# A two-layer decoder trunk on one core: first-layer scale and shift as columns by matmuls with stationary weights, in place of rows that are turned

## The reference

```python
def modulate(h, shift, scale):
    return h * (1 + scale[:, None, :]) + shift[:, None, :]

c_act = jax.nn.silu(c)
for l in range(DEPTH):
    mod = c_act @ w_ada[l] + b_ada[l]
    sh1, sc1, g1, sh2, sc2, g2, sh3, sc3, g3 = jnp.split(mod, N_MOD, axis=-1)
    h = modulate(rmsnorm(x, norm_ffn1[l]), sh1, sc1)
    x = x + 0.5 * g1[:, None, :] * swiglu(h, ffn1_w_up[l], ffn1_w_down[l])
    ...
```

## Time and profile before

| | us |
|---|---|
| median of 3 runs | 2423.11 |
| lowest and highest | 2422.92, 2424.08 |
| profiled execution, its own time | 2424.26 |
| span of the profiled execution | 2422.5 |

### The profile page before, as it was taken

How to read it: one execution, slowest core, us unless ns; L and a number is a source line. 1 busy time by engine, 2 the same in 40 slices (tenths; PEclk the granted TensorE clock), 3 DMA queues, 4 the chain that set the end, 5 groups by cost and what they waited for, 6 DMA issues and landing times.

```text
span 2422.5 us, 34408 instructions
## 1 busy us (share of the span) xinstructions
PE 2405.7 (99%) x11560; PEld 1981.8 (82%) x11560; DVE 1496.8 (62%) x2297; ACT 879.7 (36%) x1388; POOL 213.3 (9%) x159
## 2 busy tenths in 40 slices
PE   8999999999999999999999999999999999999999
PEld 6888888888888888888888888888888888888887
DVE  5777778687744577443577677877785446533332
ACT  4222223556432342222332222346653323421233
POOL 0032012000012000010300000200100111000001
PEclk9999999999999999999999999999999999999999
DMA  9666654322245346343346566533222453332332
GB/s 290 193 191 180 199 177 153 87 62 69 64 119 147 96 130 188 116 122 114 103 127 194 175 198 200 164 123 86 61 70 78 113 147 96 96 108 83 98 106 83
DMA packets 509615, 315.22 MB, mean 130 GB/s; under 512 B 9240, under 2 KB 503144, under 8 KB 508904
## 3 DMA queue, kind: packets, MB, share of 16 engines
q1 hardware_dynamic: 441376, 246.72, 35.0%
q10 hardware_dynamic: 68168, 67.62, 9.0%
HBM read 308.02 MB, written 6.29 MB: 130 GB/s over the span
## 4 chain that ended last, share of the span: by engine, by line
PE 97%; DVE 2%; ACT 0%; ACTq 0%; issue 0%
PE ps_proj L1838 28%; PE ps_proj L1839 28%; PE ps_proj L1840 28%; PE ps_mid L2074 1%; PE ps_mid L2076 1%; PE ps_mid L2075 1%; PE ps_o L2044 1%; PE ps_mid L2021 1%; PE ps_small L2033 1%; PE ps_mid L1838 1%; PE ps_mid L1840 1%; PE ps_mid L1839 1%; DVE sb_scratch L1064 1%; DVE sb_w_lo L1052 0%; PE ps_mid L2133 0%; DVE sb_h_lo L1133 0%
## 5 line engine op out<-in xcount | busy, mean ns | idle before, releaser
L1838 PE MATMUL ps_proj<-sb_a_hi,sb_w_hi 128*128 128x512 f32 x1878 | 731.2, 389 | 0.0
L1840 PE MATMUL ps_proj<-sb_a_hi,sb_w_lo 128*128 128x512 f32 x1878 | 730.7, 389 | 0.0
L1839 PE MATMUL ps_proj<-sb_a_lo,sb_w_hi 128*128 128x512 f32 x1878 | 730.6, 389 | 0.0
L609 ACT ACTIVATE sb_w_hi<-sb_raw 128x1024 fp32r<-128x1024 f32 (+1 forms) x382 | 424.5, 1111 | 829.1 <-PE ps_proj L1840 780.2
L1052 DVE TENSOR_TENSOR sb_w_lo<-sb_raw,sb_w_hi 128x1024 fp32r<-128x1024 f32 (+1 forms) x384 | 504.6, 1314 | 304.4 <-ACT sb_w_hi L609 303.6
L1838 PE MATMUL ps_proj<-sb_h_hi,sb_w_hi 128*128 128x512 f32 x1194 | 470.4, 394 | 0.1
L1840 PE MATMUL ps_proj<-sb_h_hi,sb_w_lo 128*128 128x512 f32 x1194 | 465.1, 389 | 0.0
L1839 PE MATMUL ps_proj<-sb_h_lo,sb_w_hi 128*128 128x512 f32 x1194 | 465.0, 389 | 0.0
L1840 PEld LDWEIGHTS ps_proj<-sb_a_hi,sb_w_lo 128*128 128x128 f32 x1878 | 352.4, 188 | 73.2
L1839 PEld LDWEIGHTS ps_proj<-sb_a_lo,sb_w_hi 128*128 128x128 f32 x1878 | 352.6, 188 | 73.0
L1838 PEld LDWEIGHTS ps_proj<-sb_a_hi,sb_w_hi 128*128 128x128 f32 x1878 | 352.5, 188 | 73.0
(11 more groups left out here) (297 smaller groups left out, 1938.9 us busy)
## 6 DMA issues: line engine op xcount, KB each, us to landing
sb_raw<-in_ffn_w_up SPq DMA_DIRECT2D x172, 512.0 KB, 3.8
sb_scratch<-in_w_ada ACTq DMA_DIRECT2D x128, 512.0 KB, 4.4
sb_raw<-in_w_in SPq DMA_DIRECT2D x100, 512.0 KB, 3.9
sb_raw<-in_ffn_w_down SPq DMA_DIRECT2D x64, 704.0 KB, 4.8
sb_raw<-in_w_branch_swa SPq DMA_DIRECT2D x16, 512.0 KB, 3.8
sb_raw<-in_w_branch_ret SPq DMA_DIRECT2D x16, 512.0 KB, 3.9
sb_raw<-in_w_out SPq DMA_DIRECT2D x16, 512.0 KB, 3.8
sb_scratch<-in_w_ada SPq DMA_DIRECT2D x6, 1024.0 KB, 10.5
```

The costliest lines, as they stand in the source:

```text
L609: act.activation(Whi[s][:, 0:n], raw[s][:, 0:n], ACT.Copy).then_inc(hi_ready, 1)
L1838: pe.matmul(bank, Whi[s][:, w], hi, start=first, stop=False)
L1839: pe.matmul(bank, Whi[s][:, w], lo, start=False, stop=False)
L1840: return pe.matmul(bank, Wlo[s][:, w], hi, start=False, stop=last)
```

## The change

- PE makes columns directly. `first_cols(g)` takes each 128 x 128 piece of a w_ada block as the stationary operand and one column of silu(c) as the moving one: for each of the two blocks of a group, two output columns of eight accumulating matmuls. That is 32 matmuls for a group where `first_rows` had 16, and the copies on ACT, the transposes on PE and the sums of parts on DVE are gone. `first_columns(g)` on DVE is one addition of biases for scale and shift together, read from PSUM, and one operation for the gain.
- `first_cols(g + 1)` stands where both `first_rows` of the next group stood. `first_cols(0)` stands after all turns of x.
- c is issued first on SP, ahead of x, and no more second on ACT. `idle(5)` becomes `idle(4)`.
- In the turns of x, DVE copies tiles 0, 1, 4, 5 and ACT tiles 2, 3, 6, 7 (before: even and odd ones), and the spread of 1/rms stands before tiles 6 and 7.
- In group 0, DVE makes both lo parts of the weights before the lo parts of the tiles.

```diff
-            def first_rows(n):
-
-                tile, bank = first_raw[n % FIRST_BUFS], row_banks[n % 2]
-                pe.wait_ge(first_in[n], 16)
-                if n > 1:
-                    pe.wait_ge(row_copied, n - 1)
-                for r in range(KT):
-                    a = r % ROW_GROUPS
-                    last = pe.matmul(bank[32 * a:32 * (a + 1), :], c_act[:, r:r + 1].broadcast_to([P, 32]), tile[:, 256 * r:256 * (r + 1)],
-                                     start=(r < ROW_GROUPS), stop=(r >= ROW_GROUPS))
-                last.then_inc(first_used, 1)
-
-            def turn_rows(n):
...
+            def first_cols(g):
+
+                if g:
+                    pe.wait_ge(cols_made, g)
                 else:
                     pe.wait_ge(cols_done, 1)
...
+                for kind in (SCALE, SHIFT):
+                    n = block_no(g, kind)
+                    tile = first_raw[n % FIRST_BUFS]
+                    pe.wait_ge(first_in[n], 16)
+                    for j in range(2):
+                        for r in range(KT):
+                            last = pe.matmul(pS[:, 2 * kind + j:2 * kind + j + 1], tile[:, 256 * r + P * j:256 * r + P * (j + 1)], c_act[:, r:r + 1],
+                                             start=(r == 0), stop=(r == KT - 1))
+                    last.then_inc(first_used, 1)
...
-            idle(5)
+            idle(4)
...
+            turn_x(range(4))
+            turn_vectors()
+            turn_x((4, 5))
...
             spread_rstd(0, pO, 0).then_inc(rb_ready, 1)
-            turn_rows(SCALE)
+            turn_x((6, 7))
+            first_cols(0)
             pe.wait_ge(xt_dve, KT // 2)
             pe.wait_ge(xt_act, KT // 2)
-            first_rows(SHIFT)
-            turn_rows(SHIFT)
...
                             if more:
-                                first_rows(2 * g + 2 + SCALE)
-                                first_rows(2 * g + 2 + SHIFT)
+                                first_cols(g + 1)
...
-                                elif n == 0:
-                                    turn_rows(2 * g + 2 + SCALE)
-                                    turn_rows(2 * g + 2 + SHIFT)
```

```diff
+            sp.dma_start(vec_rows[0:8, 0, :], c.rearrange("b (k p) -> (b k) p", p=P)).then_inc(c_in, 16)
             for t in range(TT):
                 sp.dma_start(xtok[:, t, :], x[0, P * t:P * (t + 1), :]).then_inc(x_in[t], 16)
...
             act.dma_start(K[:, 0:K_DECAY], consts[:, 0:K_DECAY]).then_inc(const_in, 16)
-            act.dma_start(vec_rows[0:8, 0, :], c.rearrange("b (k p) -> (b k) p", p=P)).then_inc(const_in, 16)
...
-                copy_first_row(2 * g + SCALE)
-                copy_first_row(2 * g + SHIFT)
...
+            def first_columns(g):
+
+                cols = pS[:, 0:4].rearrange("p (n j) -> p n j", n=2)
+                dve.wait_ge(first_used, 2 * (g + 1))
+                two = [a[:, 0:2 * KT].rearrange("p (n k) -> p n k", k=KT)[:, :, 2 * g:2 * g + 2] for a in (mod, vcols[:, 64:64 + 2 * KT])]
+                st.mark(dve.tensor_tensor(two[0], cols, two[1], ALU.add))
                 st.wait()
...
+                at, col = KT + 2 * g, GAIN_COL["ffn1"] + 2 * g
+                dve.scalar_tensor_tensor(gain[:, 2 * g:2 * g + 2], mod[:, at:at + 2], 1.0, vcols[:, col:col + 2], ALU.add, ALU.mult).then_inc(cols_made, 1)
+                dve.wait_ge(cols_made, g + 1)
```

More of the change, by code:

```diff
@@ L50 @@
 JOBS, FIRST_JOBS, FIRST_PAIRS = 36, 8, 2
-FIRST_BUFS, ROW_GROUPS = 4, 4
-GROUPS, SCALE, SHIFT = KT // 2, 0, 1
+FIRST_BUFS = 4
+X_DVE, X_ACT = (0, 1, 4, 5), (2, 3, 6, 7)
+GROUPS, SHIFT, SCALE = KT // 2, 0, 1
 HALF_JOBS = (JOBS - FIRST_JOBS) // 2
@@ L207, in decoder @@
         turn_banks = [pA[0], pA[1], pM[:, 0, :], pM[:, 1, :]]
-        row_banks, row_turns = [pM[:, 2 + n, 0:256] for n in range(2)], [pS[:, 256 * n:256 * (n + 1)] for n in range(2)]
         pair_banks = [pA, [pM[:, 0, :], pM[:, 1, :]]]
@@ L212, in decoder @@
         x_spill = nc.dram_tensor("x_spill", [P, KT * T], F, kind="Internal").ap()
-        const_in, vec_in, tables_in = sem("const_in"), sem("vec_in"), sem("tables_in")
+        const_in, c_in, vec_in, tables_in = sem("const_in"), sem("c_in"), sem("vec_in"), sem("tables_in")
         x_in = [sem(f"x_in{t}") for t in range(TT)]
@@ L222, in decoder @@
         first_w_in = [sem(f"first_w_in{n}") for n in range(2 * GROUPS)]
-        first_used, row_copied, row_turned, cols_made = (sem(n) for n in ("first_used", "row_copied", "row_turned", "cols_made"))
+        first_used, cols_made = sem("first_used"), sem("cols_made")
         first_w_hi, first_w_lo, xn_shifted = sem("first_w_hi"), sem("first_w_lo"), sem("xn_shifted")
@@ L347, in in_last_layer, with block_no @@
                 work()
+        def block_no(g, kind):
+            return 2 * g + (0 if kind == SCALE else 1)
         block = ctx.enter_context(nc.Block())
@@ L493, in _ @@
             st = Steps(pool, pool_step)
-            pool.wait_ge(const_in, 16 * 2)
+            pool.wait_ge(const_in, 16)
             pool.wait_ge(pos_in, 16)
@@ L841, in copy_x @@
                 act.activation(XV[:, k, :], turn_banks[k % 4][:, :], ACT.Copy).then_inc(xt_act, 1)
-            def copy_first_row(n):
-                act.wait_ge(first_used, n + 1)
-                if n > 1:
-                    act.wait_ge(row_turned, n - 1)
-                act.activation(first_row[n % 2], row_banks[n % 2], ACT.Copy).then_inc(row_copied, 1)
             def first_weights(g):
@@ L862, in _ @@
             act.activation(rs_t[:, 0:TT], rs_v[:, 0:TT], ACT.Sqrt).then_inc(first_root, 1)
-            for k in range(1, KT, 2):
+            for k in X_ACT:
                 copy_x(k)
             for g in range(GROUPS):
-                if g:
-                    first_weights(g)
-                copy_first_row(2 * g + SCALE)
-                copy_first_row(2 * g + SHIFT)
-                if g == 0:
-                    first_weights(g)
+                first_weights(g)
                 for kk in range(2):
@@ L1425, in copy_x @@
                 dve.tensor_copy(XV[:, k, :], turn_banks[k % 4][:, :]).then_inc(xt_dve, 1)
[L1427 to L1431, removed]
-                st.wait()
[L1433 to L1440, removed]
+            def first_columns(g):
[3 more added lines that the diff above has]
+                st.mark(dve.tensor_tensor(two[0], cols, two[1], ALU.add))
+                st.wait()
+                at, col = KT + 2 * g, GAIN_COL["ffn1"] + 2 * g
+                dve.scalar_tensor_tensor(gain[:, 2 * g:2 * g + 2], mod[:, at:at + 2], 1.0, vcols[:, col:col + 2], ALU.add, ALU.mult).then_inc(cols_made, 1)
+                dve.wait_ge(cols_made, g + 1)
             def scaled_x(k):
@@ L1462, in _ @@
             y, a, v = rstd[:, 0:TT], rs_t[:, 0:TT], rs_v[:, 0:TT]
-            copy_x(0)
+            for k in X_DVE[0:2]:
+                copy_x(k)
             dve.wait_ge(ssq_done, TT)
             dve.tensor_scalar(v, ssq, 1.0 / D, EPS, ALU.mult, ALU.add).then_inc(first_v, 1)
-            copy_x(2)
             dve.wait_ge(first_root, 1)
@@ L1474, in _ @@
             dve.scalar_tensor_tensor(y, a, 1.5, y, ALU.add, ALU.mult).then_inc(rstd_ready, 1)
-            copy_x(4)
-            copy_x(6)
+            for k in X_DVE[2:4]:
+                copy_x(k)
             dve.wait_ge(cols_ps, 1)
@@ L1480, in _ @@
             dve.wait_ge(xt_act, KT // 2)
+            dve.wait_ge(xt_ps, KT)
             dve.wait_ge(rb_ready, 1)
-            scaled_x(0)
             dve.wait_ge(cols_done, 1)
-            first_columns(0, SCALE)
-            scaled_x(1)
+            for k in range(2):
+                scaled_x(k)
             for g in range(GROUPS):
@@ L1489, in _ @@
                         first_weights(g, s)
-                    first_columns(g, SCALE)
-                first_columns(g, SHIFT)
+                first_columns(g)
                 st.wait()
@@ L1496, in _ @@
                 shifted_x(2 * g + 1)
-                first_lo(2 * g)
                 if g == 0:
                     first_weights(g, 1)
-                first_lo(2 * g + 1)
+                for kk in range(2):
+                    first_lo(2 * g + kk)
                 if g < GROUPS - 1:
-                    scaled_x(2 * g + 2)
-                    scaled_x(2 * g + 3)
+                    for kk in range(2):
+                        scaled_x(2 * g + 2 + kk)
             for s in range(2):
@@ L1761, in _ @@
             pe.sem_inc(y_ps, 1)
-            pe.wait_ge(const_in, 16 * 2)
+            pe.wait_ge(const_in, 16)
+            pe.wait_ge(c_in, 16)
             pe.transpose(pO[:, 0:KT], vec_rows[0:KT, 0, :], ident[0:KT, 0:KT]).then_inc(c_ps, 1)
             pe.wait_ge(c_done, 1)
-            def first_rows(n):
-                tile, bank = first_raw[n % FIRST_BUFS], row_banks[n % 2]
-                pe.wait_ge(first_in[n], 16)
-                if n > 1:
-                    pe.wait_ge(row_copied, n - 1)
-                for r in range(KT):
```

(31 more changed lines are left out.)

1 line of the change is left out of this document (removed).

## The result

The changed kernel takes 2457.99 us (median of 4 runs, 2456.27 to 2459.77) against 2423.55 us before (4 runs, 2422.92 to 2424.08). The ratio is 1.0143 with a 95% interval of 1.0130 to 1.0155. It is slower by 34.4 us, where 12.7 were forecast. The profiled execution took 2457.26 us, 33.0 more than that of before, with a span of 2455.2.

A forecast was written before the change was run, and what follows sets the result against it. PE was taken as the bound, its block behind about 50 us moving whole. Lateness 1.05 (group 0) + 7.7 (groups 1 and 2) + 3.95 (group 3) = 12.7 us gave 2435.8 us; own range 2431 to 2440, 8-in-10 range 2431 to 2460.

The forecast's parts named there:

- The sum at full clock: First unit on PE 12.7 us late, all column matmuls and products at full clock: 2435.8 us, chance 0.50.
- a period of 12.6: Groups 1 and 2 on PE: 5.45 + 7.1 + 0.25, 12.8 us each instead of 8.95.
- The wait behind group 0's block: Bias, gain and tile shift on DVE and the hi part on ACT before group 0's first product: 1.7 us.
- The first twelve products: Group 0's products on PE at 0.227 each: 2.7 us, instead of 4.45 with the clock fallen to half.
- The rival: The clock falls in the column blocks and products behind start slow: 19 us more, 2455 us, chance 0.30.
- one stretch, 2412 to 2414: End of the earlier trace: eight one-column records with the clock at 1.00, set against a fall; called short, with transposes.
- Columns: Each column block at 0.193 us a record after its first 27 records: 37 x 0.082 = 3.0 us more.
- Slow products: First twelve products behind each column block take 4.45 against 2.7 us: 1.75 more, four times.
- Its upper end: If the clock falls at once in each column block: up to 2462 us.
- The start: Up to the first columns: x's turns 0.75 us sooner, spread of 1/rms plus 0.45, columns at 15.35 instead of 15.65.
- The side gains: ACT's row copies and DVE's sums go off the path, PE's 0.74 us waits go, transfers stay covered.
- The floor of small matmuls: About 60 cycles (25 ns) a small matmul: 256 records an estimated 6.4 us instead of 28.4, sum 2413.8.

The follow-up runs named there:

- experiment 1: The changed kernel with silu(c) repeated to 64 moving columns in each column matmul, weights, loads and order the same: 2438.67 us, ratio 1.0061.
- experiment 4: The changed kernel with 128 moving columns in each column matmul instead of one: 2438.91 us, ratio 1.0061.
- experiment 3: The changed kernel with 64 moving columns and, for groups 1 to 3, column matmuls spread two behind each product of the group before: 2446.92 us, ratio 1.0086.
- experiment 5: The kernel of experiment 1 with every second column matmul left out, and so half of each sum: 2425.19 us, ratio 1.0009.

## Why the prediction was wrong

**The sum at full clock was nearly right.** It gave 12.7 us. With 64 moving columns, which is this change at full clock, the profile has the first unit 13.9 late (69.16 against 55.23), and the medians differ by 15.2. Term by term in experiment 1: columns from 16.48 (forecast 15.35; 15.41 in the changed kernel), which is nearly the whole difference of 1.2 us; 0.111 us a record at full clock (as taken from the earlier trace rows); a period of 12.6 (28.54 to 41.17, forecast 12.8). The wait behind group 0's block was 1.9 instead of 1.7. The first twelve products took the 2.8 us forecast at 2.7, but only because the clock did not fall behind that wait. The sum had dropped this fall, which the earlier trace rows has, without a reason for the clock; in experiment 4 it came and cost 1.6 us.

**The step that failed is the choice of the clock at which the sum was made.** All 256 records and all 96 products were taken at 2.4 GHz, with a chance of 0.50, and the fall of the clock stood as a rival at 0.30 and 2455 us. The rival is what happened. Against it I had put one stretch, 2412 to 2414, where eight such records left the clock at 1.00. Eight records are 0.9 us; a block here is 7. The prediction called the stretch short itself, and still chose by it. That row could not speak for the block, and it was the only thing put against a mechanism with a clear sign in the earlier trace rows, a fall of the clock after little work for the array.

**The rival's two terms, measured.** Columns: the blocks take 38.8 us in all (9.0, 10.7, 9.4, 9.8) where 256 x 0.111 is 28.4, so 10.4 for the clock; the rival had 12. Slow products: 5.0, 8.4, 8.1 and 10.4 us between the blocks and up to the first unit, against 2.8, 5.6, 5.6 and 8.3 in experiment 1, so 9.7; the rival had 7. Together 20.1, for which the rival had 19. The medians give nearly the same: 2457.99 - 2438.67 = 19.3. Within the rival, the pace at the low clock was mis-sized: 0.213 us a record, and not 0.193. I had scaled it with the length of a single load (0.33 to 0.19, a factor of 1.7), but the pace changes by 1.9. At 0.102 more a record, 10.4 us are some 25 slow records a block, where the rival had 37. So that its 12 came near is in part luck: too many slow records, each too cheap. Its upper end was also added up wrongly: with the clock low throughout each block its terms give 4 x (64 x 0.082 + 1.75) = 28, so 2463.8 and not 2462.

**The start** was forecast at 0.75 us sooner, less 0.45 for the spread. In the changed kernel silu(c) was no sooner (its table load at 5.21 against 4.97), and the columns still began within 0.1 of the forecast. That is luck: the first eight transposes of x took 0.91 from start to start there, at the pace of full clock, where they took 1.73 in experiment 1. How long the first issues on ACT take, and where the clock rises in the turns of x, differs between executions. The level in these first microseconds is read from the pace alone: the granted clock shows 1.00 there in every trace, also where the same transposes take twice as long.

**The side gains** came as forecast: no wait of 0.74, no copies, and no transfer that PE waited for behind x. They don't weigh against 28 us of loads.

**The floor of small matmuls.** The records took 28.5 us at full clock (the four blocks of experiment 1). The 60 cycles for small matmuls (the Trainium skill, "TensorE: Matmul & The Clock Gate", section "Back-to-back issue gap") would have given an estimated 6.4 us; the same section of the Trainium skill gives them for an isolated matmul, without a budget for weight loads, so they were no forecast for records that each load new weights. A record took 0.111 us at full clock and 0.213 at 1.2 GHz, its single load 0.19 and 0.33. The Trainium skill, "TensorE: Matmul & The Clock Gate", section "LDWEIGHTS (loading the stationary operand)", gives a load as its columns over 1.2 GHz, an estimated 107 ns for 128 columns, and names no clock of TensorE for it. The trace agrees with it for the pace at full clock only.

## What to carry to other kernels

A matmul with a single moving column costs its weight load, 0.11 us a record and two records in fp32, so a long matrix-by-vector product is cheaper with the vector as the stationary operand, even with the copy and the turns that this needs: 3.5 us of PE's time a group here (the period of 8.95 less 5.45 of products, a wait of 0.7 included) against 7.1. A busy PE isn't enough to keep its clock: long runs of weight loads with hardly any moving data cost this kernel 19.3 us through the clock on top of the 15.2 that the change costs at full clock, for the matmuls behind them too, and repeating the moving column removed that for nothing. Before evidence is set against a fall of the clock, its length should be compared with that of the stretch it is to speak for.

## What the runs showed of the hardware that I had not expected

- The clock fell from 1.00 to 0.50 with PE busy throughout, within the first block of columns and again in each of the next three. With 64 or 128 moving columns in the same instructions it stayed at 1.00 in the blocks.
- A mixture of one 512-column product and four records of 64 columns stayed at whichever clock it met, in the one trace of it: at 0.50 from 26 to 43.8 us and then, after a few plain products, at 1.00 to its end. The four runs fall into two groups, one of 2438.5 us (granted clock 0.999) and three about 2447 (0.995).
- Spreading records of weight loads between products hid no load beyond the one that each product hides anyway: a product with four records took 0.227 + 4 x 0.111.
- The same wait of 1.9 us behind group 0's block was followed by a fall of the clock in experiments 3, 4 and 5 and not in experiment 1. Twelve plain products behind it brought the clock back (experiment 4).
- 128 moving columns in fp32 were as free beneath a weight load as 64 (2438.91 against 2438.67 us).
